# State-space stage of a hybrid encoder on one core: u and y change layout by on-chip transfers instead of a round trip through scratch

## The reference, cut to what matters

```
u = (h @ w_in).reshape(B, S, G, C)                  # 64 groups of 16 channels
x_s = a * x_(s-1) + b @ u_s                         # 64 complex states a group
y = c_re @ x_re - c_im @ x_im + d_skip * u
y = gelu(y)
val, gate = split(y @ w_glu, 2)
return val * sigmoid(gate)
```

## Time and profile before

| | |
|---|---|
| median of 3 runs | 1100.39 us (1098.67 to 1102.09) |
| the profiled execution | 1102.55 us, of which the profile's span is 1100.7 us |
| TensorE busy | 1086.2 us, 99% of the span |
| TensorE weight loads (beside the matmuls) | 891.6 us, 81% |
| VectorE busy | 785.0 us, 71% |
| ScalarE busy | 476.1 us, 43% |
| mean granted clock of TensorE | 0.996 of full speed |

### The profile page before, as it was taken

The page is one execution under the profiler, slowest core; times in us unless marked ns, Lnnn a source line. Parts: engine busy times, 40 slices in busy tenths (PEclk is TensorE's granted clock), DMA queues, the critical chain, the costliest instruction groups (busy, mean ns, idle before and its releaser), DMA issues.

```text
span 1100.7 us, 15912 instructions
## 1 busy us (share of the span) xinstructions
PE 1086.2 (99%) x6180; PEld 891.6 (81%) x6180; DVE 785.0 (71%) x1171; ACT 476.1 (43%) x744; POOL 63.1 (6%) x162
## 2 busy tenths in 40 slices
PE   9999999999999999999999989999999999999997
PEld 6778878888888888888887778888888888888886
DVE  6869848688787788978868866557774467655765
ACT  6557734444324543345452223344442244413453
POOL 1383031000000000000000000000000000000000
PEclk9999999999999999999999989999999999999999
DMA  7332214233233333333287843222223233235622
GB/s 234 108 112 81 68 38 135 77 115 133 97 128 122 115 115 110 124 113 124 86 277 218 247 140 118 96 96 96 96 96 101 99 101 100 79 114 138 144 88 91
DMA packets 81546, 131.25 MB, mean 119 GB/s; under 512 B 39040, under 2 KB 49024, under 8 KB 81472
## 3 DMA queue, kind: packets, MB, share of 16 engines
q1 hardware_dynamic: 71856, 123.69, 35.4%
q0 software_dynamic: 1152, 4.19, 1.1%
q10 hardware_dynamic: 8464, 2.36, 0.9%
HBM read 111.02 MB, written 14.88 MB: 114 GB/s over the span
## 4 chain that ended last, share of the span: by engine, by line
PE 92%; DVE 3%; DMA 2%; DVEq 1%; issue 1%; ACT 1%; SPq 0%; ACTq 0%
PE bank L1774 27%; PE bank L1775 27%; PE bank L1776 27%; PE bank L1980 2%; DMA ud_scratch<-UB 2%; PE bank L2077 1%; PE bank L2079 1%; PE bank L2078 1%; PE bank L1965 1%; DMA YB<-yd_scratch 1%; PE bank L2044 1%; PE bank L1846 1%; PE bank L1955 0%; PE bank L1953 0%; PE bank L1952 0%
## 5 line engine op out<-in xcount | busy, mean ns | idle before, releaser
L614 ACT ACTIVATE WH<-RAW 128x1024 fp32r<-128x1024 f32 (+1 forms) x169 | 175.8, 1042 | 343.0 <-PE bank L1776 328.1
L1774 PE MATMUL bank<-GH,WH 128*128 128x512 f32 x816 | 320.7, 393 | 0.0
L1776 PE MATMUL bank<-GH,WL 128*128 128x512 f32 x816 | 317.7, 389 | 0.0
L1775 PE MATMUL bank<-GL,WH 128*128 128x512 f32 x816 | 317.5, 389 | 0.0
L1032 DVE TENSOR_TENSOR WL<-RAW,WH 128x1024 fp32r<-128x1024 f32 (+1 forms) x169 | 202.8, 1201 | 35.5 <-ACT WH L614 35.0
L1774 PE MATMUL bank<-AH,WH 128*128 128x512 f32 x532 | 209.1, 393 | 4.3 <-DVE AL L1561 3.4
L1776 PE MATMUL bank<-AH,WL 128*128 128x512 f32 x532 | 207.4, 390 | 0.0
L1775 PE MATMUL bank<-AL,WH 128*128 128x512 f32 x532 | 207.3, 390 | 0.0
L1774 PEld LDWEIGHTS bank<-GH,WH 128*128 128x128 f32 x816 | 153.1, 188 | 32.6 <-issue 0.7
L1776 PEld LDWEIGHTS bank<-GH,WL 128*128 128x128 f32 x816 | 153.2, 188 | 32.2
L1775 PEld LDWEIGHTS bank<-GL,WH 128*128 128x128 f32 x816 | 153.2, 188 | 31.9 <-issue 0.7
(11 more groups left out here) (299 smaller groups left out, 1050.1 us busy)
## 6 DMA issues: line engine op xcount, KB each, us to landing
RAW<-in_w_up SPq DMA_DIRECT2D x88, 512.0 KB, 3.3
RAW<-in_w_dn SPq DMA_DIRECT2D x32, 512.0 KB, 3.2
RAW<-in_w_glu SPq DMA_DIRECT2D x16, 512.0 KB, 3.3
RAW<-in_w_dn SPq DMA_DIRECT2D x16, 384.0 KB, 3.1
RAW<-in_w_wo SPq DMA_DIRECT2D x8, 512.0 KB, 3.4
od_scratch<-OO SPq DMA_DIRECT2D x8, 512.0 KB, 3.3
kd_scratch<-KT SPq DMA_DIRECT2D x8, 512.0 KB, 4.5
O<-od_scratch POOLq DMA_DIRECT2D x8, 512.0 KB, 6.4
```

The costliest lines, as they stand in the source:

```text
L614: act_(w_hi(b)[:, :n], RAW[b % RW][:, :n], ACT.Copy).then_inc(s_hi, 1)
L1774: mm(out, wh, hi_[:, k, :], start=start, stop=False)
L1775: mm(out, wh, lo_[:, k, :], start=False, stop=False)
L1776: return mm(out, wl, hi_[:, k, :], start=False, stop=stop)
```

## The change

Each scratch round trip becomes eight transfers, one for each group of 16 channels, straight from one place in on-chip memory to another: sixteen for a tile. u's are issued by SP, y's by ACT; both scratch arrays and SP's `u_in` and `y_in` go. The completion counts become 16 x 8 a tile. ACT's `y_out` now also waits until `YB` has been read (`y_lo` of tile j - 2), which SP did. The tables of tiles 5 and 7 get places of their own, over the part of `ET` that `inputs` has used, so they are loaded when E says so and no longer when Y does; `TM` 4, 5 and 7 are issued one round earlier. In the gated blocks, column 3 of blocks 0 and 1 is done after `outputs(5)` and three columns of block 1; on DVE, `y_lo(4)` stands ahead of `states(7)`.

```diff
-PLACE_FREE = {3: 1, 5: 2, 7: 4}
-LAGS_AT = {2: 4, 3: 3, 5: 5, 6: 7}
+LAGS_AT = {1: 4, 3: 3, 4: 5, 5: 7}
...
-        for j, i in ((3, 0), (5, 1), (7, 0)):
-            TM[j], O2[j] = TM[i], O2[i]
+        TM[3], O2[3] = TM[0], O2[0]
+        for j in (5, 7):
+            TM[j], _ = place(f"TM{j}", [P, 2 * QJ, C * LQ], F32, A0 + 4096 * (j - 5))
+            O2[j], _ = place(f"O2{j}", [P, 2, QJ, C * LQ], F32, A0 + 4096 * (j - 4))
...
+        def group(i):
+            return slice(C * i, C * i + C)
+        def u_landed(j):
+            return s_ur[j % 3], 16 * GJ * (j // 3 + 1)
+        def y_landed(j):
+            return s_yr[j % 2], 16 * GJ * (j // 2 + 1)
...
+            def place_free(j):
+                if j == 3:
+                    sp.wait_ge(s_Y, 1)
+                if j in (5, 7):
+                    sp.wait_ge(s_E, j - 3)
...
+            def u_out(j):
+                sp.wait_ge(s_ev, nth(FIRST["win"] + j))
+                if j >= 3:
+                    sp.wait_ge(s_Y, j - 2)
+                for i in range(GJ):
+                    sp.dma_start(U2[j % 3][:, i, :], UB[j % 2][group(i)]).then_inc(s_ur[j % 3], 16)
+
             for t in range(NJ):
                 u_out(t)
-                u_in(t)
-                if t >= 3:
-                    y_in(t - 3)
                 load(FIRST["win"] + 5 + t)
                 if t in LAGS_AT:
                     lags_in(LAGS_AT[t])
-            for j in range(NJ - 3, NJ):
-                y_in(j)
...
             def y_out(j):
                 act.wait_ge(s_g, j + 1)
-                nc.scalar.dma_start(cmaj(YD[j]), Y2[j % 2][:]).then_inc(s_yw[j % 2], 16)
+                if j >= 2:
+                    act.wait_ge(s_act, TILE0["y"] + j - 1)
+                for i in range(GJ):
+                    nc.scalar.dma_start(YB[j % 2][group(i)], Y2[j % 2][:, i, :]).then_inc(s_yr[j % 2], 16)
...
             states(NJ - 2)
+            y_lo(NJ - 4)
             states(NJ - 1)
-            y_lo(NJ - 4)
...
-            pool.wait_ge(s_ur[2], 16)
+            pool.wait_ge(*u_landed(1))
             fetch(4)
-            for j in (3, 5, 7):
-                pool.wait_ge(s_Y, PLACE_FREE[j])
+            pool.wait_ge(s_Y, 1)
+            fetch(3)
+            for j in (5, 7):
+                pool.wait_ge(s_E, j - 3)
                 fetch(j)
...
-            glu_part((0,), range(4))
+            glu_part((0,), range(3))
             inputs(NJ - 2)
             outputs(NJ - 3)
-            glu_part((1,), range(4))
+            glu_part((1,), range(3))
+            glu_part((0, 1), (3,))
             inputs(NJ - 1)
             outputs(NJ - 2)
```

More of the change, by code:

```diff
@@ L348, in build @@
         KD_ = nc.dram_tensor("kd_scratch", (NJ, P, LQ, C * LQ), F32, kind="Internal").ap()
-        UD = nc.dram_tensor("ud_scratch", (NJ, P, LQ, NK), F32, kind="Internal").ap()
         TD = nc.dram_tensor("td_scratch", (3, P, P), F32, kind="Internal").ap()
-        YD = nc.dram_tensor("yd_scratch", (NJ, P, LQ, NK), F32, kind="Internal").ap()
         s_raw = [sem(f"raw{i}_loaded") for i in range(RW)]
@@ L375, in build @@
         s_tmr, s_or = [sem(f"TM{j}_loaded") for j in range(NJ)], [sem(f"O{j}_loaded") for j in range(NJ)]
-        s_uw, s_ur = sem("ud_written"), [sem(f"U{i}_loaded") for i in range(3)]
+        s_ur = [sem(f"U{i}_spread") for i in range(3)]
         s_rt, s_E, s_X, s_Y, s_g = sem("RT"), sem("E"), sem("states"), sem("Y"), sem("gelu")
-        s_yw, s_yr = [sem("even_yd_written"), sem("odd_yd_written")], [sem("YB0_loaded"), sem("YB1_loaded")]
+        s_yr = [sem("YB0_spread"), sem("YB1_spread")]
         s_sig = sem("sigmoid")
@@ L428, in span @@
             return range(FIRST[name], FIRST[name] + BLOCKS[name])
-        def cmaj(dram):
-            return bass.AP(dram.tensor, dram.offset, [[NK, P], [C * LQ * NK, GJ], [1, NK]])
+        def group(i):
[4 more added lines that the diff above has]
+            return s_yr[j % 2], 16 * GJ * (j // 2 + 1)
         @block.sync
@@ L554, in lags_in @@
                 sp.wait_ge(s_kw, 16 * (j + 1))
-                if j in PLACE_FREE:
-                    sp.wait_ge(s_Y, PLACE_FREE[j])
+                place_free(j)
                 sp.dma_start(TM[j][:], bass.AP(k.tensor, k.offset, [[C * LQ, P], [C * LQ * P, GJ], [1, C * LQ]])
@@ L948, in gelu @@
                 if j >= 2:
-                    act.wait_ge(s_yw[j % 2], 16 * (j // 2))
+                    act.wait_ge(*y_landed(j - 2))
                 for gi in range(2):
@@ L956, in y_out @@
                 act.wait_ge(s_g, j + 1)
-                nc.scalar.dma_start(cmaj(YD[j]), Y2[j % 2][:]).then_inc(s_yw[j % 2], 16)
+                if j >= 2:
+                    act.wait_ge(s_act, TILE0["y"] + j - 1)
+                for i in range(GJ):
+                    nc.scalar.dma_start(YB[j % 2][group(i)], Y2[j % 2][:, i, :]).then_inc(s_yr[j % 2], 16)
             def y_tile(j):
-                act.wait_ge(s_yr[j % 2], 16 * (j // 2 + 1))
+                act.wait_ge(*y_landed(j))
                 act_(AH[:, j, :], YB[j % 2][:].rearrange("p s k -> p (s k)"), ACT.Copy).then_inc(s_thi, 1)
@@ L1522, in u_out @@
                 if j >= 2:
-                    dve.wait_ge(s_uw, 16 * (j - 1))
+                    dve.wait_ge(*u_landed(j - 2))
                 v.tensor_tensor(UB[j % 2][:], bank[BANK[b]][:].rearrange("p (k s) -> p s k", s=LQ),
@@ L2085, in inputs @@
             def inputs(j):
-                pe.wait_ge(s_ur[j % 3], 16 * (j // 3 + 1))
+                pe.wait_ge(*u_landed(j))
                 if j == 0:
```

## The result

The change made the kernel slower: 1108.11 us median of 4 runs (1107.50 to 1112.40) against 1100.30 of before (1098.67 to 1102.09); the ratio is 1.0084, 95% interval 1.0067 to 1.0102. That is 11.3 us above the forecast and 3.1 above the end of its range. The profiled execution took 1108.61 us for a span of 1106.8; that of before took 6.06 us less.

What follows compares the result with a forecast made beforehand. TensorE, busy 99%, was taken as the bound. First tiles 0 plus gated blocks 3.6 us (6.31 removed, 2.9 added, 0.2 saved) gave 1096.8 us; own range 1094.5 to 1099.5, with rivals 1092 to 1105.

Steps and rivals of the forecast that it cites:

- The price of an issue: On SP's and ACT's queues: 0.60 us per issue, eight taking 4.75 us, the tile landing 6.1 us after the first.
- Rival (2): SP's and ACT's queues can't issue at once: 1.6 us in each of five loop rounds, 1104.8 us; chance 0.18.
- first sign of being wrong: On either queue: the forecast is wrong if issues are outside 0.5 to 0.7 us.
- The first tiles: 576 to 612 us: u tile 2 waits 1.3 us, u tile 3's 1.3 us wait goes, so they count nothing.
- Rival (3): First tiles: u tile 2 comes 2.9 us late, the clock costs 2.9 more, total 1099 to 1102 us; chance 0.18.
- The loop: TensorE's 8.79 us per tile: ACT's 7.5 us fits, DVE runs about 0.5 us later, no cost.
- The gated blocks: From 627.61 us: 6.31 us removed, 2.9 added by three new waits, 0.2 saved on switches, a gain of 3.6 us.
- (b): Gated blocks: TensorE waits 1.05 us for the states of tile 7, behind DVE's low part of y tile 4.
- (a): Gated blocks: TensorE waits 0.9 us for u tile 7, written at 634.1 and landing 6.1 us later.
- (c): Gated blocks: TensorE waits 0.95 us for the low part of y tile 6, behind ACT's issues, table load and copy.
- I charge them no clock: Gated blocks: the three new waits, each under 1.4 us, cost no slow clock, as 1.3 us idle earlier left it at 1.00.
- rival (4): A queue's pieces don't overlap: 16 us a tile, 36 us more in five loop rounds, 1133 us; chance 0.02.

Runs made afterwards that it cites:

- the fastest of the kernels above: The change, with POOL issuing four of each u and y tile's eight pieces and SP fetching O 4, 3, 5 and 7: 1095.71 us, ratio 0.9972.

## Why the prediction was wrong

The price of an issue held, nearly: SP's eight stand 0.64 us apart, ACT's 0.65, for 0.60 forecast, and a piece lands in 2.1 us where nothing is ahead. But one issue of a tile, at times two, takes 1.1 to 1.4 us, so that eight take 5.0 to 6.0 us on SP and 5.1 to 6.0 on ACT, not 4.75. Rival (2), the queues taking turns, is not what this is. Around 626 us both queues issue side by side at their usual price (fastest, median and slowest in ns):

```profile
L567 SPq DMA_DIRECT2D U<-UB x6: 592/598/603, 623.9 to 627.0; - x6
L958 ACTq DMA_DIRECT2D YB<-Y x8: 555/622/708, 624.1 to 628.7; - x8
```

and of the ten long pieces five come while no other engine issues (at 599.86, 608.20, 622.48, 640.54 and 651.58). What they have in common is in the last section. So the prediction's first sign of being wrong, issues outside 0.5 to 0.7 us, came true for single ones; its second, SP's issues stretching where ACT's run, does not tell where they are.

**The first tiles: the step that failed.** "I take a wait of 1.3 us, from 0 to 2.9", and no clock. Measured 4.19 and 2.72 for the clock, 5.6 us more than charged; "u 2 is over 3 us late" was a sign that the prediction had named. The step had u 2's pieces from 587.2 on (587.93) and the tables as what was ahead of them, rightly; but it let u 2 land by 598 and it landed at 599.92. It had counted 2.75 MB, u 2's own among them, at 300 GB/s. From 587 to 599.92 3.74 MB moved, at 289 GB/s: y 0's pieces (0.25 MB, from 592.21), the weight load behind u 2 (0.5 MB, 593.83) and the first pieces of u 3 (597.21) were not in its count. And u 2's last piece went out at 593.15, some 1.8 us after the forecast's, 0.7 of it by the long issue at 591.78. How much each of these cost is not shown. Rival (3), u 2 late and the clock down, named this, and was sized too small. u 0 and u 1, "nothing to 1 us" and "the same", took 0.50 and 0.52. The removal was right: u 3's wait is gone, and the 1.33 without a releaser with it.

**The loop: "no cost" was nearly right**: 0.53 us, for u 5. Its condition for a delay that grows, a price above about 0.63, was just met (0.64 to 0.65), but u 6 waited hardly more, 0.56.

**The gated blocks.** AL at k = 3 is in time and the clock there at 1.00, as forecast. That wait of u 6 was not in the forecast. Of the new waits (b) X 7 was right, 1.05 and measured 0.96, and so was its way: DVE waits for ACT's copy 4, then does AL 4 and the nine of `states(7)`. (a) u 7 was forecast at 0.9 and took 2.19: SP's eight took 6.03 us and the last piece 2.75, 7.7 from first issue to landing where 6.1 was charged. (c) AL 6 was forecast at 0.95 and took 1.91: the chain of issues, table load and copy behind GELU 7 is as drawn, each piece a little longer. "I charge them no clock" failed for AL 6, 1.69 us; that it held for u 7 was luck, as its reason, waits under 1.4 us, did not hold there.

The sum again, with what was measured: the forecast -3.6; u 2 +5.6; u 0 and u 1 +1.0; u 5 and u 6 +1.1; u 7 +1.3; AL 6 +1.0 and +1.7; the 1.33 saved -1.3. That makes +6.8 for a measured 6.06 between the profiled executions. The ways on which the prediction waited were the right ones. What failed was sizes, above all the wait of a tile whose issue is held up until the tables go out, and the clock that follows, which it put at nothing.

The Trainium skill (DMA: Bandwidth & Descriptors, Rules for kernel authors) advises to coalesce small transfers. The change was slower, but not as rival (4) priced that advice: the page does not say that one piece waits for another, and taken one after another they would have cost 36 us. The trace shows them overlapping, landing in 2.1 us where nothing is ahead, and the fastest of the kernels above makes the same 128 transfers from one more queue.

## What to carry to other kernels

Replacing a round trip by many small transfers moves the cost from waiting to issuing: count the time for which the issues hold their queue, and ask what stands behind them on it and what traffic they then meet. If a queue is full, look for an idle engine that can issue half: here that was worth 8 us, where moving the other traffic was worth nothing. A price that is right to 7% per issue still leaves the wait open by microseconds when the transfers land in a stretch at a DMA share of 1.

## What the runs showed of the hardware that was not expected

**Long issues go with transfers on the instruction queue.** All ten pieces of the changed kernel that took 1.07 to 1.43 us to issue overlap a transfer of 16 KB on the queue that the profile calls "instruction"; the 107 pieces that overlap none took at most 0.88 us. Eleven more overlap one and are not long. For the piece issued at 622.48, in the window 622.4 to 623.9:

```profile
q1 hardware_dynamic: 144, 0.03, 16.9%
q8 instruction: 1, 0.02, 4.0%
```

That the one makes the other long was not tried.

**The idle time alone did not tell whether the granted clock fell**: 1.91 us for AL 6 were followed by 0.52, while 2.19 for u 7 of the same run, 2.67 in the kernel with the new order alone and 2.99 with the first tiles split were not followed by any fall. Executions of one kernel differ too: of 29 of the kernel before, the six fastest (1096.58 to 1097.55 us) had a mean clock of 0.999, and those at 0.996 took 1100.11 us and more. So the one profile of a kernel does not tell how often a wait of it costs the clock, and the parts that the clock has in the sums above are those of one execution.

**POOL's late issues.** POOL's own issue is 0.53 us, but at some places it stood still without a releaser that the profile names. Its timeline in the fastest kernel:

```profile
605.01 1.60 POOL L1782 DMA_DIRECT2D U<-UB  x3 [1.99 <-DVE UB L1533]
608.75 0.52 POOL L1782 DMA_DIRECT2D U<-UB  x1 [2.14 <-issue]
609.33 1.59 POOL L1775 DMA_DIRECT2D YB<-Y  x3
612.70 0.54 POOL L1775 DMA_DIRECT2D YB<-Y  x1 [1.77 <-issue]
```

From 602.50 to 629.75 every fourth issue is 0.8 to 3.0 us late there. Each of these seven comes 0.35 us behind the landing of the transfer that POOL had issued four before it: the piece of 602.50 landed at 608.40, that of 608.75 at 612.35. The kernel with u and y split and POOL's own fetches shows the same, 0.35 us, at 602.41, 609.53, 615.74, 621.09 and 624.68. Four is not general: with y's eight pieces on POOL the last piece of y 1 was 1.73 us late and that of y 2 4.80. What sets the number was not settled.
